# A decoder layer with a mixture of experts on one core: two state write-backs, two output weight tiles and the last norm rearranged

## The reference, cut to what matters

```python
def _layer_norm(x, g, b):
    mu = x.mean(-1, keepdims=True)
    var = jnp.square(x - mu).mean(-1, keepdims=True)
    return (x - mu) * lax.rsqrt(var + LN_EPS) * g + b

def step(s, qkv):                                  # retention; s is the state of a sample
    s = c_dec * s + jnp.einsum('bhjd,bhje->bhde', kc * k_dec, vc)
    ...

def _post_block(x, feats, w_o, ln1_g, ln1_b, moe, ln2_g, ln2_b):
    h = _layer_norm(DEEPNORM_ALPHA * x + feats @ w_o, ln1_g, ln1_b)
    return _layer_norm(DEEPNORM_ALPHA * h + _hmoe(h, *moe), ln2_g, ln2_b)
```

## Time and profile before

| | |
|---|---|
| median of 3 runs | 1653.22 us (1653.11 to 1659.95) |
| the profiled execution, own time | 1652.81 us |
| its span, first to last instruction | 1651.0 us |
| around the span | 1.81 us |
| TensorE busy | 1359.7 us, 82% |
| VectorE busy | 591.1 us, 36% |
| ScalarE busy | 281.1 us, 17% |
| chain of waits: transfers | 40% of the span |
| chain of waits: TensorE | 23% of the span |
| mean granted clock | 0.916 |

### The profile page before, as it was taken

One profiled execution on the slowest core, in us unless ns is written; L12 is line 12 of the kernel. 1 busy time (PEld: TensorE's weight loads), 2 busy tenths in 40 slices (PEclk: granted clock), 3 DMA queues, 4 the chain that ended last, 5 costly groups with the idle time before them and its releaser, 6 DMA issues.

```text
span 1651.0 us, 24641 instructions
## 1 busy us (share of the span) xinstructions
PE 1359.7 (82%) x10641; PEld 846.8 (51%) x10641; DVE 591.1 (36%) x1263; ACT 281.1 (17%) x659; POOL 89.4 (5%) x112
## 2 busy tenths in 40 slices
PE   8999999999998799986865877668787576686675
PEld 6887888888865577742322333223332232232332
DVE  2845567687686121283401212012030120120125
ACT  0022301201364010131010111101111011011113
POOL 1220011010232000010000000000000000000000
PEclk9999999999999899998888989888898788797798
DMA  9985486897699898469999999999999999999996
GB/s 347 378 280 196 158 287 223 300 336 262 248 378 423 304 290 328 153 262 415 427 428 426 428 420 426 428 426 427 399 429 426 428 426 428 427 425 428 426 427 254
DMA packets 139874, 591.24 MB, mean 358 GB/s; under 512 B 9056, under 2 KB 98672, under 8 KB 106864
## 3 DMA queue, kind: packets, MB, share of 16 engines
q1 hardware_dynamic: 122624, 497.70, 75.8%
q0 software_dynamic: 10432, 75.82, 11.8%
q10 hardware_dynamic: 6704, 16.08, 2.5%
HBM read 580.54 MB, written 17.45 MB: 362 GB/s over the span
## 4 chain that ended last, share of the span: by engine, by line
DMA 40%; PE 23%; DVE 1%; ACT 1%; issue 0%; DVEq 0%; SPq 0%
DMA arena<-in_w_up 38%; PE ps L2188 9%; PE ps L2129 7%; PE ps L2206 3%; PE ps L2157 2%; DMA arena<-in_w_down 1%; DMA arena<-in_w_o 1%; PE ps L2163 1%; PE ps L2120 1%; ACT arena L1663 1%; PE ps L2215 0%; PE ps L2116 0%; PE ps L2344 0%; PE ps L2248 0%; ACT arena L1731 0%
## 5 line engine op out<-in xcount | busy, mean ns | idle before, releaser
L2188 PE MATMUL ps<-arena 128*32 128x256 f32 x4352 | 343.5, 486 | 239.3 <-DMA arena<-in_w_up 237.7
L2188 PEld LDWEIGHTS ps<-arena 128*32 128x32 f32 x4352 | 185.2, 138 | 412.1 <-issue 366.5
L687 PE MATMUL ps<-arena 128*128 128x264 f32 x1600 | 365.5, 386 | 0.4 <-ACT arena L382 0.4
L687 PEld LDWEIGHTS ps<-arena 128*128 128x128 f32 x1600 | 299.8, 190 | 50.4 <-issue 1.7
L1922 DVE TENSOR_TENSOR arena<-arena,ps 64x256 f32<-64x256 f32 x34 | 14.4, 425 | 480.9 <-ACT arena L1667 480.9
L2129 PE MATMUL ps<-arena 128*128 128x264 f32 x512 | 121.3, 395 | 6.8 <-PEq L2413 4.8
L2206 PE MATMUL ps<-arena 128*32 128x512 f32 x1088 | 124.1, 595 | 0.6 <-ACT arena L1671 0.4
L2129 PEld LDWEIGHTS ps<-arena 128*128 128x128 f32 x512 | 97.4, 193 | 29.8 <-issue 11.2
L1667 ACT ACTIVATE arena<-ps 64x256 f32<-64x256 f32 x34 | 12.8, 375 | 571.8 <-PE ps L2188 571.8
L2157 PE MATMUL ps<-arena 128*32 128x512 f32 (+1 forms) x816 | 98.5, 595 | 1.0 <-DVE arena L1871 1.0
L1680 ACT COPY arena<-ps 32x512 f32<-32x512 f32 x128 | 73.7, 576 | 134.2 <-PE ps L2206 122.4
(11 more groups left out here) (483 smaller groups left out, 1093.0 us busy)
## 6 DMA issues: line engine op xcount, KB each, us to landing
arena<-in_w_gate SPq DMA_DIRECT2D x60, 2048.0 KB, 31.1
arena<-in_w_up SPq DMA_DIRECT2D x60, 2048.0 KB, 34.1
arena<-in_w_down SPq DMA_DIRECT2D x59, 2048.0 KB, 31.3
arena<-in_w_in SPq DMA_DIRECT2D x50, 1024.0 KB, 10.3
arena<-in_w_o SPq DMA_DIRECT2D x16, 1024.0 KB, 11.1
arena<-in_w_down SPq DMA_DIRECT2D x10, 1024.0 KB, 31.1
arena<-in_w_up SPq DMA_DIRECT2D x8, 1024.0 KB, 33.4
arena<-in_w_gate SPq DMA_DIRECT2D x8, 1024.0 KB, 27.4
```

Of the source, the lines that this page charges most:

```text
L687: last = pe.matmul(ps[:, n % 2, 0:T], ring[:, slot, k, cols], x[:, k, :], start=(k == 0), stop=(k == KT - 1))
L2188: last = pe.matmul(ps[BS * q:BS * q + BS, 0, 0:CHUNK // 2], xs[:, kk * 4 + i, :], w[:, at:at + CHUNK // 2], start=(k == 0), stop=(k == KT ...
```

## The change

Four edits.

1. `N_EARLY` is 2: SP starts two tiles of `w_o` before it leaves `phase_s`, and the write-backs of states 6 and 7 behind them. These two count in a semaphore of their own, `state_kept`, which is not among those cleared between the blocks. SP doesn't wait for them there, but in `phase_m`, behind the last tile of `w_o` and ahead of the first expert's weights (expert 0 goes to the slot in which the two states lay).
2. The row sums of the last norm are taken in two parts. ACT sums the old `sums_y` of both tiles (`old_total`, 128x2048 each) in the last block, ahead of that block's activation. The last block's own share follows by linearity: ACT's copy of it to `yq` also sums its columns (`y_total`), and TensorE multiplies that column by the gates (2 products of one column). DVE adds the two (`less`).
3. The sums themselves stay in PSUM: for all 8 chunks (2 tiles, 4 chunks) TensorE adds old sum and own rows, one chunk after the other. ACT squares each chunk from PSUM and DVE takes the mean off from PSUM, each as soon as the chunk is there, DVE behind ACT. The products of the samples' statistics stand between the chunks.
4. The samples' last four elementwise steps go from DVE to POOL.

```diff
-N_EARLY = 1
+N_EARLY = 2
...
         def state_out(u):
             sp.wait_ge(S["s_st_new"], u + 1)
-            sp.dma_start(by_run(o["s_ret"][0, u]), s_old[u % 3].rearrange("p d e -> p (d e)")).then_inc(st_out[u % 3], 16)
+            sp.dma_start(by_run(o["s_ret"][0, u]), s_old[u % 3].rearrange("p d e -> p (d e)")
+                         ).then_inc(st_out[u % 3] if u < 6 else m.state_kept, 16)
...
-        project_in(sp, a, m, 0)
+        for n in range(N_EARLY):
+            project_in(sp, a, m, n)
         for b in (6, 7):
             state_out(b)
-        for n in (0, 1):
-            sp.wait_ge(st_out[n], 16 * len(range(n, NS_TOK, 3)))
         sp.wait_ge(front["kv_out"], 160)
         sp.wait_ge(front["win_moved"], 32)
...
             for c in range(N_EARLY, n_wo):
                 project_in(sp, a, m, c)
+            sp.wait_ge(m.state_kept, 32)
             for e in range(NE):
...
+            pool.wait_ge(S["f_lnq"], 128)
+            pool.wait_ge(S["f_smv"], 1)
+            pool.wait_ge(S["f_dev"], 1)
+            pool.tensor_scalar(acc_s, acc_s, s_nmean, None, ALU.add).then_inc(S["f_sm"], 1)
+            pool.wait_ge(S["f_sm"], 1)
+            pool.tensor_tensor(acc_s, acc_s, ln_rows[:, 0, :], ALU.mult).then_inc(S["f_sm"], 1)
+            pool.wait_ge(S["f_sm"], 2)
+            pool.wait_ge(S["f_srs"], 1)
+            pool.tensor_scalar(acc_s, acc_s, s_rstd, None, ALU.mult).then_inc(S["f_sm"], 1)
+            pool.wait_ge(S["f_sm"], 3)
+            pool.tensor_tensor(acc_s, acc_s, ln_rows[:, 1, :], ALU.add).then_inc(S["f_so"], 1)
...
+            def old_total(t):
+                A.activation(ye, sums_y[:, t], ACT.Copy, accum_out=total[:, t:t + 1]).then_inc(S["f_total"], 1)
...
+                    for t in (0, 1):
+                        act.wait_ge(S["d_paired"], 4 * t + 4)
+                        if t:
+                            act.wait_ge(S["f_total"], 1)
+                        old_total(t)
                 hidden(b)
...
-            A.copy(yq[1], ps[:, 4, :]).then_inc(S["f_y"], 1)
+            A.activation(yq[1], ps[:, 4, :], ACT.Copy, accum_out=y_total).then_inc(S["f_y"], 1)
...
-            def totals(t):
-                for c in range(4):
...
-                A.activation(squares, sums_y[:, t], ACT.Square, bias=less[:, t:t + 1], accum_out=spread_of[:, t:t + 1]).then_inc(S["f_sq"], 1)
...
+            def deviation(t):
                 for c in range(4):
+                    if t and c == 2:
+                        act.wait_ge(S["f_var"], 1)
+                        A.activation(s_rstd, ps[:, 7, 1:2], ACT.Sqrt, bias=r_("eps")).then_inc(S["f_sstd"], 1)
                     chunk = slice(c * CHUNK, (c + 1) * CHUNK)
...
+                    act.wait_ge(S["f_comb"], 4 * t + c + 2)
+                    A.activation(ye[:, chunk], ps[:, 4 * t + c, :], ACT.Square, bias=less[:, t:t + 1], accum_out=parts[:, t, c:c + 1]).then_inc(S["f_sq"], 1)
+                act.wait_ge(S["f_sq"], 4 * t + 4)
+                A.activation(shares[:, t, 0:4], parts[:, t, :], ACT.Copy, scale=1.0 / D, accum_out=spread_of[:, t:t + 1]).then_inc(S["f_var_t"], 1)
...
             def less_mean(t):
...
-                v.scalar_tensor_tensor(centred, sums_y[:, t], less[:, t:t + 1], ln2[0], ALU.add, ALU.mult).then_inc(S["f_sub"], 1)
+                for c in range(4):
+                    chunk = slice(c * CHUNK, (c + 1) * CHUNK)
+                    v.wait_ge(S["f_comb"], 4 * t + c + 2)
+                    v.wait_ge(S["f_sq"], 4 * t + c + 1)
+                    last = v.scalar_tensor_tensor(centred[t][:, chunk], ps[:, 4 * t + c, :], less[:, t:t + 1], ln2[0][:, chunk], ALU.add, ALU.mult)
+                last.then_inc(S["f_sub"], 1)
...
+            v.wait_ge(S["f_lin"], 1)
+            v.scalar_tensor_tensor(less, ps[:, 6, 0:2], -1.0 / D, less_old, ALU.mult, ALU.add).then_inc(S["f_less"], 1)
...
             less_mean(1)
-            v.wait_ge(S["f_lnq"], 128)
             v.wait_ge(S["f_sstd"], 1)
-            v.reciprocal(s_rstd, s_rstd)
-            done.link(v.scalar_tensor_tensor(acc_s, acc_s, s_nmean, ln_rows[:, 0, :], ALU.add, ALU.mult))
-            v.scalar_tensor_tensor(acc_s, acc_s, s_rstd, ln_rows[:, 1, :], ALU.mult, ALU.add).then_inc(S["f_so"], 1)
+            v.reciprocal(s_rstd, s_rstd).then_inc(S["f_srs"], 1)
             normed(1)
...
+                for t in (0, 1):
+                    last = pe.matmul(ps[:, 6, t:t + 1], sel_q[1][:, t * P:(t + 1) * P], y_total, start=True, stop=True)
+                last.then_inc(S["f_lin"], 1)
+                own_samples(7, 1).then_inc(S["f_comb"], 1)
+                for t in (0, 1):
+                    for c in range(4):
+                        bank = 4 * t + c
...
+                        pe.matmul(ps[:, bank, :], ident, sums_y[:, t, c * CHUNK:(c + 1) * CHUNK], start=True, stop=False)
+                        own_rows(bank, 1, t, c, False).then_inc(S["f_comb"], 1)
```

More of the change, by code:

```diff
@@ L1508, in phase_m @@
     assert all(last_use[s] < final_first for s in own)
-    ln2, squares, centred = [ring[:, s] for s in own[0:2]], ring[:, own[3]], ring[:, own[4]]
+    ln2, centred = [ring[:, s] for s in own[0:2]], [ring[:, s] for s in own[3:5]]
     ends = Taker(arena, own[2] * SLOT, (own[2] + 1) * SLOT)
     yq, sel_q = [ends(CHUNK), ends(CHUNK)], [ends(T_WIDE), ends(T_WIDE)]
-    shares, total, less, spread_of = ends(2, 8), ends(2, 4), ends(2), ends(2)
+    shares, total, less, spread_of = ends(2, 8), ends(2), ends(2), ends(2)
+    parts, less_old, y_total = ends(2, 4), ends(2), ends(1)
     def over_slot(c):
@@ L1721, in _ @@
             act.wait_ge(*down_done(final))
[L1722 removed]
+            A.activation(yq[1], ps[:, 4, :], ACT.Copy, accum_out=y_total).then_inc(S["f_y"], 1)
             over(0)
+            with act.If(n_over > 0):
+                act.wait_ge(S["f_more"], 1)
+                act.wait_ge(S["f_total"], 2)
+                old_total(0)
+                act.wait_ge(S["f_total"], 3)
+                old_total(1)
             A.activation(shares[:, 0, 4:5], r_("eps"), ACT.Sqrt)
[L1726 removed]
+            act.wait_ge(S["f_total"], 2)
@@ L1731, in totals @@
-                    A.activation(squares[:, chunk] if t == 0 else sums_y[:, 1, chunk], src, ACT.Copy, accum_out=total[:, t, c:c + 1]).then_inc(S["f_total"], 1)
-                act.wait_ge(S["f_total"], 4 * t + 4)
-                A.activation(shares[:, t, 0:4], total[:, t, :], ACT.Copy, scale=-1.0 / D, accum_out=less[:, t:t + 1]).then_inc(S["f_less"], 1)
-            def deviation(t):
-                act.wait_ge(S["f_less"], t + 1)
-                A.activation(squares, sums_y[:, t], ACT.Square, bias=less[:, t:t + 1], accum_out=spread_of[:, t:t + 1]).then_inc(S["f_sq"], 1)
-                act.wait_ge(S["f_sq"], t + 1)
-                A.activation(rstd[:, t:t + 1], spread_of[:, t:t + 1], ACT.Sqrt, scale=1.0 / D, bias=r_("eps")).then_inc(S["f_std"], 1)
@@ L1742, in _ @@
+            act.wait_ge(S["f_less"], 1)
             deviation(0)
             act.wait_ge(S["f_mean"], 1)
-            A.activation(s_nmean, ps[:, 1, 0:1], ACT.Copy, scale=-1.0).then_inc(S["f_dev"], 1)
+            A.activation(s_nmean, ps[:, 7, 0:1], ACT.Copy, scale=-1.0).then_inc(S["f_dev"], 1)
             act.wait_ge(S["f_dev"], 1)
             A.activation(s_dev, s_mv[:, 0:1], ACT.Square, bias=s_nmean).then_inc(S["f_dev"], 1)
-            totals(1)
-            act.wait_ge(S["f_var"], 1)
@@ L1749, in _ @@
-            A.activation(s_rstd, ps[:, 1, 1:2], ACT.Sqrt, bias=r_("eps")).then_inc(S["f_sstd"], 1)
             deviation(1)
@@ L2341, in last_sums @@
                 pe.wait_ge(S["f_y"], 1)
-                def second_sum(c):
-                    pe.matmul(ps[:, SUM_BANK + c, :], ident, sums_y[:, 1, c * CHUNK:(c + 1) * CHUNK], start=True, stop=False)
-                for c in range(4):
-                    last = own_rows(c, 1, 0, c, True)
-                last.then_inc(S["f_comb"], 1)
-                second_sum(0)
-                pe.wait_ge(S["f_add"], 1)
-                own_samples(SAMPLE_BANK, 1).then_inc(S["f_comb"], 1)
-                for c in range(1, 4):
-                    second_sum(c)
@@ L2354, in last_sums @@
-                for c in range(4):
-                    own_rows(SUM_BANK + c, 1, 1, c, False).then_inc(S["f_comb"], 1)
-                pe.wait_ge(S["f_add"], 2)
-                pe.wait_ge(S["f_smv"], 1)
-                pe.matmul(ps[:, 1, 0:1], same, s_mv[:, 0:1], start=True, stop=True).then_inc(S["f_mean"], 1)
-                pe.wait_ge(S["f_dev"], 2)
-                pe.matmul(ps[:, 1, 1:2], same, s_mv[:, 1:2], start=True, stop=False)
-                pe.matmul(ps[:, 1, 1:2], same, s_dev, start=False, stop=True).then_inc(S["f_var"], 1)
+                for t in (0, 1):
+                    last = pe.matmul(ps[:, 6, t:t + 1], sel_q[1][:, t * P:(t + 1) * P], y_total, start=True, stop=True)
@@ new lines, in last_sums @@
+                last.then_inc(S["f_lin"], 1)
[3 more added lines that the diff above has]
```

(15 more changed lines are left out.)

28 lines of the change are left out of this document (13 added, 15 removed).

## The result

| | before | after |
|---|---|---|
| median, runs on the same chips | 1653.16 us (20 runs) | 1657.63 us (20 runs) |
| the profiled execution | 1652.81 us | 1657.59 us |
| its span | 1651.0 us | 1655.8 us |

The ratio of the runs is 1.002, with a 95% interval of 1.0011 to 1.0029: 3.3 us slower, between 1.8 and 4.8. That is also the difference of the means; the medians differ by 4.5. The spans of the two profiled executions differ by 4.8 us. They split at ACT's copy of the last expert's result, which stood at 1630.17 and stands at 1626.97 now: the front gained 3.2 us by then, and the tail behind it took 28.8 instead of 20.8 us, 8.0 more.

The account below looks back on a forecast made before the run. It took TensorE to set the pace from about 559 to 750 us, then weight transfers, then a tail without loads. 1652.81 - 4.4 (front) + 7.1 (tail) + 0.4 (median) gave 1655.9 us, range 1650 to 1660.

Parts of the forecast that it names:

- Two regimes, both counted in full: TensorE sets the pace from about 559 to 750 us, then transfers; gains there and tail changes move the end fully.
- the 4 to 5 named as a sign: At the end of the weight stream: the last weights land 4 to 5 us earlier.
- The border, 1.9 (1.3 to 2.7): At the block's end before w_o: dropping SP's wait for the write-backs gains 1.9 us, between 1.3 and 2.7.
- The second tile, 1.9: At the start of w_o: TensorE's 1.9 us wait for the second tile goes, as it is asked for earlier.
- The clock, 0.6: At TensorE's first w_o products: shorter idleness ahead means less time at half clock, 0.6 us gained.
- Front, 4.4: Border, second tile and clock at the start of w_o together gain 4.4 us, from 3.2 to 7.0.
- The pairs, 2.1 each, and the scaling of tile 1 done 24.5 behind ACT's copy: In the tail: each old-sum and own-rows pair on TensorE takes 2.1 us, eight take 16.9, delaying tile 1's scaling.
- The first rival: In the tail's pairs: single own rows cost 0.27 us beside identity products, giving 1648.8 us; chance 0.08.
- ACT's sums of the old rows, nothing: In the last block: ACT's two sums, 2.00 us each, cost nothing because ACT waits for weights there.
- POOL, 0.2: At the tail's end: POOL's last two sample steps take 2 us, finish with tile 1, and add 0.2 us.
- The rival in which POOL and DVE take turns: At the tail's end: POOL's steps and DVE's halves exclude each other, ending 2 us later, 1658.5 us; chance 0.13.
- A half clock in the tail: Rival: TensorE's last 19.7 us run at clock 0.50, costing up to 17 us more, 1673 us; chance 0.04.

Follow-up runs that it names:

- e10: e8 with the write-backs of states 6 and 7 issued behind the sixth w_o tile and the samples' steps behind tile 1's scaling; 1647.38 us, ratio 0.9967.
- e1: The kernel before with only the two early w_o tiles and the later wait for the last two write-backs; 1650.68 us, ratio 0.9975.
- e2: The changed kernel with the old front: one w_o tile early, all write-backs waited for in the block; 1664.52 us, ratio 1.0068.
- e3: The changed kernel with the samples' last four steps taken from POOL and done as two on DVE; 1657.63 us, ratio 1.0013.
- e7: The changed kernel with each own-rows product of the last sums taking all 128 rows, which alters the computation; 1655.28 us, ratio 0.9994.
- e8: The changed kernel with tile 0's old sums ahead of the last result, other sums grouped, samples' steps on DVE; 1650.31 us, ratio 0.9973.
- e9: The same kernel as e3, run once more; 1654.87 us (one run).
- e6: The kernel before with the last two write-backs waited for in the next block, but only one w_o tile early; 1652.74 us, ratio 0.9988.
- e5: The changed kernel with POOL's first two steps waiting for tile 0's scaling and its last two for tile 1's; 1660.71 us, ratio 1.0042.
- e4: The changed kernel with TensorE's last sums in groups of identity products and own rows, one pair left, instead of eight pairs; 1653.8 us, ratio 0.9994.

## Why the prediction was right, step by step

The forecast was 2.7 us slower, the traces say 4.8, the runs 3.3 (1.8 to 4.8). The direction and both mechanisms were right. Of the 2.1 us by which the traces lie above the forecast, 1.2 are the front (3.2 gained, not 4.4) and 0.9 the tail (8.0 lost, not 7.1). The prediction also held that so small a difference can't be told from none; twenty runs of each kernel did tell it. One reading in it is too wide: the last of the 40 slices moves 254 GB/s, not 399 or more, but it is the tail, and no term rests on it.

- *Two regimes, both counted in full.* Right. From the end of `w_o` to ACT's last copy it is 935.1 us before and 936.0 in the changed kernel, and 934.4 to 936.9 in all twelve profiles, so what TensorE gained by the end of `w_o` (3.3 to 5.8 us in the nine with edit 1's front or e10's) moved the whole stream, but for this scatter. By their traces the front in e1 and the tail in e2 add up to the whole. The last weights landed 3.2 us sooner (1614.97 instead of 1618.13), less than the 4 to 5 named as a sign.
- *The border, 1.9 (1.3 to 2.7).* In the changed kernel's profile it was 1.1, because the values of sample 7 ran at half clock (2.80 instead of 1.93) and ACT's copy came last. Where they ran at the full clock (e1, e3, e7, e8, e9) it was 1.7 to 2.5, and there SP's held issue came last, by 0.3 to 1.1 us over ACT's copy. In all of them the first `w_o` instruction follows the last arrival by 1.8 to 1.9. e10 takes the held issue away and gets 2.8. So the value taken, between a free and a held issue, fits where the clock stayed up; that a low clock would delay ACT's copy was not in the sum.
- *The second tile, 1.9.* Right, the wait is gone; by e6's trace the border's gain depends on it.
- *The clock, 0.6.* From the first `w_o` instruction to the end of `w_o` it is 132.80 instead of 135.75; less the 1.94 of the tile, 1.0: the term was low by 0.4.
- *Front, 4.4.* 4.07 at the end of `w_o`, 3.2 at the last result. The first expert's low clock, which the sum didn't have, took 1.5, and 0.6 came back by the last result. It is not the change's work: the same 128 instructions take 8.44 to 8.80 in ten of twelve profiles, the old front of e2 among them, and 7.11 in before and e7 alone. The profiled execution against which the sum was made was a lucky one there. How much of that loss reaches the end is not shown: e7, without the low clock there, has 936.7 us from `w_o` to the last copy, and e9, with 8.80, has 934.4.
- *The pairs, 2.1 each, and the scaling of tile 1 done 24.5 behind ACT's copy.* Right: 2.1, and 24.6 in the changed kernel, 24.1 without POOL (e9). That 32 rows among full ones cost what 128 cost, weighed there against the row of four, is what e7 shows. The first rival is out.
- *ACT's sums of the old rows, nothing.* No cost is seen: in e2, which has them and the old front, the stretch from `w_o` to the last copy is 934.5 us, 935.1 before.
- *POOL, 0.2.* This step failed. Its two last steps were put at 2 us, from two copies, and as ending with tile 1. They take 2.84 alone (e5) and 3.91 beside DVE, and slow DVE by 0.44 as well: 1.5 us at the end (e9). The rival in which POOL and DVE take turns was the better account, with a price of 1.5 instead of 2.6; a term of 1.5 in the sum would have given 1657.2.
- *A half clock in the tail.* Not in the changed kernel's profile, but it exists: e3's last two pairs, 4 us.
- *The clock* remains unexplained in three places. In the tail it fell in e3 and not in e9, the same kernel. At the first expert TensorE had been busy for only 0.4 us of the last 2 ahead of it, in all twelve profiles, and the clock was low in ten. At the values of sample 7 it was low in after, e4 and e5, each time behind a wait of 0.47 to 0.58 us for the sample's pages (`in_sel_v`); e3 has such a wait (0.45) and no low clock, and the other eight have neither. What decides it was not tried.

## What to carry to other kernels

Here a product on a quarter of TensorE's rows was cheap only next to others on the other quarters (four together 1.07 to 1.14 us, one among full products 1.05): count the groups, not the products, and bring the products that don't need the last result ahead of it. Work given to another engine to relieve one that isn't last is not free when both read the same memory at that moment (1.5 us here). And a wait that is removed at a border can turn up again at the load behind it, if that isn't moved too (e6's trace).

## What the runs showed of the hardware

- A held issue (the engine that starts a transfer is kept at it while earlier ones are under way): SP needed 2.2 to 2.6 us to issue two write-backs of 512 KB behind one tile of 1 MB, and 4.1 to 4.8 behind two.
- DVE and POOL: POOL's step with a per-row number on 128x512 takes 1.58 us alone, its sum of two such tiles 1.26 (e5). Beside DVE's two halves of 1024 columns (1.28 each alone) it matters who began. In tile 0 POOL began 0.02 us ahead and kept its times, and DVE's halves took these:

```profile
1639.51 1.74 DVE L2104 SCALAR_TENSOR_TENSOR arena<-arena 128x1024 f32<-128x1024 f32 x1
```

```profile
1641.17 2.32 DVE L2104 SCALAR_TENSOR_TENSOR arena<-arena 128x1024 f32<-128x1024 f32 x1
```

  In tile 1 DVE began 0.08 ahead, and POOL's 1.58 became 2.65: it ended 1.44 behind DVE's first half, so it was held for nearly all of that half. DVE's second half then took 1.71. The Trainium skill, "SBUF — State Buffer", Who interferes with whom, says that a DVE instruction with two inputs in SBUF contends with a GpSimd one that reads there, that the ports the two share are an exclusive lock, and that the order of issue decides who blocks. The trace agrees where DVE began. Where POOL began, DVE yielded, but not for the whole of POOL's instructions: it lost 0.5 beside one of 1.58 and 1.0 beside one of 1.26 (1.74 and 2.32 instead of 1.28).
- The clock can fall to 0.50 while TensorE is busy without a pause (e3, at 1642.7), and did not in five other profiles of the same pairs or of pairs with full rows (after, e2, e5, e9, e7).
